# Gather, turn and scatter two experts' rows at a time: one list of 128 rows on 128 partitions

## The reference, cut to what matters

```
expert = g_sel[:, None] * EXPERTS_PER_GROUP + top_idx        # two per token
def expert_block(args):
    tok, e = args
    xb = x_pad[tok]                                          # gather rows
    hdn = jax.nn.silu(xb @ w1[e]) * (xb @ w3[e])             # 1024 -> 256
    return hdn @ w2[e]                                       # 256 -> 1024
y = y.reshape(R, D) * buf_w[:, None]                         # gate
return jnp.zeros((N + 1, D), xf.dtype).at[buf_tok].add(y)[:N]
```

## Time and profile before

| | us |
|---|---|
| median of three runs | 1641.41 |
| profiled execution, its own time | 1641.72 |
| its span | 1639.9 |
| PE busy in the span | 1408.5 |
| POOL busy in the span | 159.9 |

### The profile page before, as it was taken

The page is one execution under the profiler, slowest core; times in us unless marked ns, Lnnn a source line. Parts: engine busy times, 40 slices in busy tenths (PEclk is TensorE's granted clock), DMA queues, the critical chain, the costliest instruction groups (busy, mean ns, idle before and its releaser), DMA issues. The chain is left out here.

```text
span 1639.9 us, 21516 instructions
## 1 busy us (share of the span) xinstructions
PE 1408.5 (86%) x8567; PEld 1005.1 (61%) x8567; DVE 578.3 (35%) x1281; ACT 562.8 (34%) x1055; POOL 159.9 (10%) x193
## 2 busy tenths in 40 slices
PE   4999999999999988878797999699887879888760
PEld 4888887787888855555585888455444444444430
DVE  5455565334311415666463455211010101001007
ACT  5434444222322444454310465233222222222223
POOL 0000000000000000000000111322212121212110
PEclk9999999999999979999899999799999888899995
DMA  5101111113233300000464872999999999999977
GB/s 156 52 26 40 30 36 39 30 39 103 77 118 106 90 1 1 1 1 1 165 235 143 310 246 102 354 383 371 392 382 388 387 385 389 376 381 383 375 276 307
DMA packets 138211, 314.64 MB, mean 192 GB/s; under 512 B 32241, under 2 KB 86513, under 8 KB 120705
## 3 DMA queue, kind: packets, MB, share of 16 engines
q1 hardware_dynamic: 125056, 288.06, 49.1%
q0 software_dynamic: 13056, 25.23, 4.5%
HBM read 284.86 MB, written 43.02 MB: 200 GB/s over the span
## 5 line engine op out<-in xcount | busy, mean ns | idle before, releaser
L2031 PE MATMUL ps<-r,m_xT 128*64 128x256 f32 x2048 | 270.2, 423 | 77.7 <-DMA r<-in_w 76.4
L129 PE MATMUL ps<-uTh,h_wh 128*128 128x512 f32 (+3 forms) x696 | 264.5, 380 | 7.5 <-DVE uTl L546 7.5
L2031 PEld LDWEIGHTS ps<-r,m_xT 128*64 128x64 f32 x2048 | 158.2, 152 | 171.4 <-DMA r<-in_w 84.4
L130 PE MATMUL ps<-uTl,h_wh 128*128 128x512 f32 (+3 forms) x696 | 256.7, 369 | 0.0
L131 PE MATMUL ps<-uTh,h_wl 128*128 128x512 f32 (+3 forms) x696 | 256.5, 368 | 0.0
L129 PEld LDWEIGHTS ps<-uTh,h_wh 128*128 128x128 f32 (+1 forms) x696 | 130.1, 187 | 31.8 <-DVE uTl L546 8.3
L1993 DVE TENSOR_TENSOR m_prod<-m_sig,ps 128x128 f32<-128x128 f32 x64 | 18.4, 288 | 358.5 <-ACT m_sig L1955 278.8
L131 PEld LDWEIGHTS ps<-uTh,h_wl 128*128 128x128 f32 (+1 forms) x696 | 130.0, 187 | 20.1
L130 PEld LDWEIGHTS ps<-uTl,h_wh 128*128 128x128 f32 (+1 forms) x696 | 130.3, 187 | 19.4 <-issue 0.2
L2050 PE MATMUL ps<-r,m_hT 128*64 128x512 f32 x512 | 123.9, 605 | 0.4 <-issue 0.4
L1966 ACT ACTIVATE rows<-ps,gate 64x512 f32<-64x512 f32 x128 | 87.3, 682 | 87.1 <-PE ps L2050 85.5
(11 more groups left out here) (325 smaller groups left out, 2051.3 us busy)
## 6 DMA issues: line engine op xcount, KB each, us to landing
r<-in_w SPq DMA_DIRECT2D x192, 1024.0 KB
h_w<-in_w_in SPq DMA_DIRECT2D x37, 512.0 KB, 4.1
gates<-h_sg POOLq DMA_DIRECT2D x16, 512.0 KB, 2.9
e_gate<-gates SPq DMA_DIRECT2D x16, 512.0 KB
r<-y_moe SPq DMA_DIRECT2D x8, 1024.0 KB, 12.5
e_wo<-in_w_out SPq DMA_DIRECT2D x4, 1024.0 KB
merged<-e_m SPq DMA_DIRECT2D x8, 512.0 KB
f_m<-merged SPq DMA_DIRECT2D x8, 512.0 KB, 6.7
```

The source lines that it names most:

```text
L129: pe.matmul(out, lh, rh, start=start, stop=False)
L130: pe.matmul(out, lh, rl, start=False, stop=False)
L2031: ins = pe.matmul(bank(UP_BANK + e % 2, 0, DE, CAP * f, CAP * (f + 1)).rearrange("p (r f) -> p r f", r=2), xT[e % 2][:, j, :], g.r13[b][:, ...
```

## The change

Experts 2i and 2i + 1 become pair i. One gather brings the rows of both, the even one's on partitions 0 to 63 and the odd one's on 64 to 127; one set of eight transposes turns all 128 rows into two PSUM banks; two ACT copies take them out (one bank each); the two products stay per expert and read 64 of the 128 columns each; the results go to partitions 0 to 63 and 64 to 127 of a tile of their own, and one scatter sends both. Row tiles and result tiles are three each. DVE makes `g.src` and `g.dst` in two halves each, so the first gather waits for two instructions. Two gathers of 128 rows are issued ahead in place of three of 64. Left out below: sizes and declarations, and the same edit of `g.dst`.

```diff
-XB = 5
+XB = 3
+PAIRS = EXPERTS // 2
...
-            dve.tensor_scalar(g.src[:, :], LISTS(0, EXPERTS), SKIP, None, ALU.add).then_inc(rows_ok, 1)
+            halves = [(k, slice(k * CAP, (k + 1) * CAP)) for k in range(2)]
+            for k, part in halves:
+                dve.tensor_scalar(g.src[part, :], LISTS(0, EXPERTS)[part, k::2], SKIP, None, ALU.add).then_inc(rows_ok, 1)
...
-            for e in range(EXPERTS + 2):
+            for i in range(PAIRS + 1):
+                n = i + XB - 1
+                if n < PAIRS:
+                    if n >= XB:
+                        pool.wait_ge(x_tr, n - XB + 1)
+                    settle(pool, g)
+                    pool.indirect_dma_start(out=x[n % XB], out_offset=None, in_=g.u2,
+                                            in_offset=bass.IndirectOffsetOnAxis(ap=g.src[:, n:n + 1], axis=0),
...
+                if i >= 1:
+                    n = i - 1
+                    pool.wait_ge(y_ok, 4 * n + 4)
+                    settle(pool, g)
+                    pool.indirect_dma_start(out=g.y, out_offset=bass.IndirectOffsetOnAxis(ap=g.dst[:, n:n + 1], axis=0),
+                                            in_=y[n % XB][:, :], in_offset=None,
...
+            def copied(i):
+                act.wait_ge(x_tr, i + 1)
+                if i >= 2:
+                    act.wait_ge(up_mm, 2 * (i - 2) + 2)
+                for q in range(2):
+                    act.activation(xT[i % 2][:, 4 * q:4 * q + 4, :], bank(X_BANK + q).rearrange("p (j t) -> p j t", j=4),
+                                   ACT.Copy).then_inc(xT_ok, 1)
...
+                if e % 2 == 0 and e // 2 + 1 < PAIRS:
+                    copied(e // 2 + 1)
...
+            def turn(i):
+                pe.wait_ge(x_in[i % XB], 16 * (i // XB) + 16)
+                settle(pe, g)
+                if i:
+                    pe.wait_ge(xT_ok, 2 * i)
+                for j in range(DK):
+                    ins = pe.transpose(bank(X_BANK + j // 4, j % 4 * P, P), x[i % XB][:, j::DK], g.ident[:, :])
+                ins.then_inc(x_tr, 1)
...
-                                            xT[e % 2][:, j, :], g.r13[b][:, :, j, HALF * f:HALF * (f + 1)],
+                                            xT[i % 2][:, j, CAP * k:CAP * (k + 1)], g.r13[b][:, :, j, HALF * f:HALF * (f + 1)],
...
+                if e % 2 == 0 and e // 2 + 1 < PAIRS:
+                    turn(e // 2 + 1)
```

More of the change, by code:

```diff
@@ L1429, in output_part @@
         io8, io128, tok, upper = sb("f_io8", [P, 8]), sb("f_io128", [P, 2, EXPERTS]), sb("f_tok", [P, TT]), sb("f_upper", [P, P])
-        srcf = sb("f_srcf", [P, EXPERTS])
+        srcf = sb("f_srcf", [P, PAIRS])
         fill, xr, xr_in = g.fill, g.xrow, g.x_in
@@ L1530, in gpsimd @@
             pool.wait_ge(filled, 16 * FILLS)
-            for b in range(AHEAD):
-                pool.memset(xr[b], 0.0).then_inc(z_ok, 1)
+            for i in range(XB - 1):
+                pool.memset(xr[i], 0.0).then_inc(z_ok, 1)
             def record(t):
@@ L1543, in gpsimd @@
                 record(t)
-            pool.wait_ge(z_ok, AHEAD)
-            pool.wait_ge(rows_ok, 1)
+            pool.wait_ge(z_ok, XB - 1)
+            pool.wait_ge(rows_ok, 2)
             pool.wait_ge(u_out, 16 * TT)
             settle(pool, g)
[L1548 to L1551, removed]
+            for i in range(XB - 1):
+                pool.indirect_dma_start(out=xr[i], out_offset=None, in_=g.u2,
+                                        in_offset=bass.IndirectOffsetOnAxis(ap=g.src[:, i:i + 1], axis=0),
+                                        bounds_check=SEQ - 1, oob_is_err=False).then_inc(xr_in[i], 16)
             record(TT - 1)
@@ L1723, in vector @@
             dve.wait_ge(oh_mm, TT)
-            dve.tensor_scalar(g.src[:, :], LISTS(0, EXPERTS), SKIP, None, ALU.add).then_inc(rows_ok, 1)
-            c.mark(dve.tensor_scalar(srcf[:, :], LISTS(0, EXPERTS), SKIP, None, ALU.add))
+            halves = [(k, slice(k * CAP, (k + 1) * CAP)) for k in range(2)]
+            for k, part in halves:
+                dve.tensor_scalar(g.src[part, :], LISTS(0, EXPERTS)[part, k::2], SKIP, None, ALU.add).then_inc(rows_ok, 1)
+            for k, part in halves:
+                c.mark(dve.tensor_scalar(srcf[part, :], LISTS(0, EXPERTS)[part, k::2], SKIP, None, ALU.add))
             dve.tensor_copy(g.gate[:, :], LISTS(EXPERTS, EXPERTS)).then_inc(rows_ok, 1)
             dve.wait_ge(dv, c.now())
-            dve.scalar_tensor_tensor(out=g.dst[:, :], in0=srcf[:, :], scalar=2.0, in1=LISTS(2 * EXPERTS, EXPERTS),
-                                     op0=ALU.mult, op1=ALU.add).then_inc(rows_ok, 1)
+            for k, part in halves:
+                dve.scalar_tensor_tensor(out=g.dst[part, :], in0=srcf[part, :], scalar=2.0,
+                                         in1=LISTS(2 * EXPERTS, EXPERTS)[part, k::2], op0=ALU.mult, op1=ALU.add).then_inc(rows_ok, 1)
             dve.wait_ge(rk_mm, TT + 1)
@@ L1818, in experts_part @@
         sb = lambda n, s, d=F32: here.enter_context(nc.sbuf_tensor(n, s, d))
-        x, y, x_in = g.xrow, g.y_tile, g.x_in
-        xT = [sb(f"m_xT{b}", [P, DK, CAP]) for b in range(2)]
+        x, x_in = g.xrow, g.x_in
+        xT = [sb(f"m_xT{b}", [P, DK, P]) for b in range(2)]
         sig = [sb(f"m_sig{b}", [P, HALF]) for b in range(2)]
+        y = [g.y_first] + [sb(f"m_y{b}", [P, D]) for b in range(1, XB)]
         prod, hid = sb("m_prod", [P, HALF]), sb("m_hid", [P, HALF])
@@ L1828, in experts_part @@
         h_tr, hT_ok, dn_mm, y_ok = sem("m_h_tr"), sem("m_hT_ok"), sem("m_dn_mm"), sem("m_y_ok")
-        late_x, late_sig, late_prod, late_hid, late_y = x[0], x[1][:, 0:DE], x[2][:, 0:DE], x[3][:, 0:DE], x[4]
-        late_xT, late_hT = xT[0], hT
+        late_x, late_y = x[0][0:CAP, :], y[0][0:CAP, :]
+        late_sig, late_prod, late_hid = (t[0:CAP, 0:DE] for t in (x[1], x[2], y[1]))
+        late_xT, late_hT = xT[0][:, :, 0:CAP], hT
         rec, late_rows = sb("v_rec", [CAP, ROWS]), sb("v_rows", [CAP, ROWS], I32)
@@ L1909, in gpsimd @@
         def gpsimd(pool):
-            for b in range(AHEAD, XB):
-                pool.memset(x[b], 0.0).then_inc(x_zero, 1)
-            pool.wait_ge(x_zero, XB - AHEAD)
-            for e in range(EXPERTS + 2):
[L1914 to L1917, removed]
-                    settle(pool, g)
[L1919 to L1924, removed]
+            pool.memset(x[XB - 1], 0.0).then_inc(x_zero, 1)
@@ new lines, in gpsimd @@
+            pool.wait_ge(x_zero, 1)
+            for i in range(PAIRS + 1):
[3 more added lines that the diff above has]
+                        pool.wait_ge(x_tr, n - XB + 1)
+                    settle(pool, g)
+                    pool.indirect_dma_start(out=x[n % XB], out_offset=None, in_=g.u2,
+                                            in_offset=bass.IndirectOffsetOnAxis(ap=g.src[:, n:n + 1], axis=0),
+                                            bounds_check=SEQ - 1, oob_is_err=False).then_inc(x_in[n % XB], 16)
+                if i >= 1:
+                    n = i - 1
+                    pool.wait_ge(y_ok, 4 * n + 4)
@@ L1925, in gpsimd @@
                     settle(pool, g)
-                    pool.indirect_dma_start(out=g.y, out_offset=bass.IndirectOffsetOnAxis(ap=g.dst[0:CAP, e - 2:e - 1], axis=0),
-                                            in_=y[b], in_offset=None,
-                                            bounds_check=2 * SEQ - 1, oob_is_err=False).then_inc(y_out[b], 16)
+                    pool.indirect_dma_start(out=g.y, out_offset=bass.IndirectOffsetOnAxis(ap=g.dst[:, n:n + 1], axis=0),
+                                            in_=y[n % XB][:, :], in_offset=None,
+                                            bounds_check=2 * SEQ - 1, oob_is_err=False).then_inc(y_out[n % XB], 16)
@@ L1929, in gpsimd @@
             pool.wait_ge(g.rec_out, 32 * TT)
             for b in range(XB):
-                pool.wait_ge(y_out[b], 16 * len(range(b, EXPERTS, XB)))
+                pool.wait_ge(y_out[b], 16 * len(range(b, PAIRS, XB)))
             pool.sem_inc(v_turn, 1)
@@ L1951, in scalar @@
         def scalar(act):
-            for e in range(-1, EXPERTS + 1):
-                if 0 <= e < EXPERTS:
+            def copied(i):
[5 more added lines that the diff above has]
+                                   ACT.Copy).then_inc(xT_ok, 1)
+            copied(0)
+            for e in range(EXPERTS + 1):
+                if e < EXPERTS:
                     act.wait_ge(up_mm, e + 1)
                     act.activation(sig[e % 2][:, :], bank(UP_BANK + e % 2, 0, HALF), ACT.Sigmoid).then_inc(sig_ok, 1)
[L1956 to L1959, removed]
+                if e % 2 == 0 and e // 2 + 1 < PAIRS:
+                    copied(e // 2 + 1)
                 if e >= 1:
-                    b = (e - 1) % XB
-                    if e - 1 >= XB:
-                        act.wait_ge(y_out[b], 16 * ((e - 1) // XB))
+                    i, k = (e - 1) // 2, (e - 1) % 2
```

(23 more changed lines are left out.)

## The result

The kernel after takes 1601.15 us (median; 1599.30 to 1602.21) against 1641.34 for the kernel before: ratio 0.9754, 95% interval 0.9737 to 0.9771. It is 40 us faster, where 1642.6 and a range of 1633 to 1650 were predicted. The profiled execution took 1602.19 us, span 1600.5.

A forecast was written before the change was run, and what follows sets the result against it. The prediction took the DMA engines' stream of 201 MB of weights and the rows to bound the loop. Terms -0.6 + 1.0 + 0.5 + 0.3 = +1.2 on 1641.4 gave 1642.6 us, range 1633 to 1650.

The forecast's parts named there:

- What bounds the kernel now: Whole loop: as long as the DMA engines need for 201 MB of weights and the rows, at a share of 1.02.
- Bytes: Gathers and scatters: same rows moved, 64 transfers with their completions go; -0.6 us, gain bounded at 1.7.
- Split of a list of 128: Rows of a 128-place list dealt over 16 engines: +1 us taken, from -15 (even) to +28 (eight consecutive places).
- Transposes, ACT, POOL: Loop: PE saves 33 us in transposes, ACT copies as before, POOL saves 60 us of issues; all hidden, 0 each.
- Start: First "up" later by 0.8 to 5 us, say 3; hidden by weights already queued, so 0.
- Tail: After the last weights: last "up" possibly slower, 0 to 3.0 us, +0.5 taken; last scatter with both experts, +0.3.
- D: Rival, faster: rows go where the late engines get fewer, gain ends at 8 to 11 us, 1632 us; chance 0.10.
- E: Rival, faster: the chain's PE pieces to 1146 us are a real bound, 1634 us; chance 0.05.
- a last weight that lands over 4 us earlier: Loop's end: a sign that the forecast is wrong; if right, expert 63's weights land at about the same us.

The follow-up runs named there:

- e1: The changed kernel with each gather of 128 rows put back into two of 64, to partitions 0 to 63 and 64 to 127: 1640.38 us, ratio 0.9997.
- f3: The kernel before with separate row and result tiles, three each, and each one-expert gather naming 128 places, 64 skipped: 1600.96 us; its control, with 64-place lists, 1631.22.
- g2: The changed kernel with the places of each expert's list permuted so that filled places spread over all short runs of four: 1591.50 us, ratio 0.9706.
- g3: The kernel before with the places of each expert's list permuted so that filled places spread over all short runs of four: 1633.56 us, ratio 0.9967.
- e4: The changed kernel with every place of the gathers' lists out of range, so gathers run without rows: 1574.79 us; first weight loads left at 1019 to 1025 over all profiled runs.
- e2: The changed kernel with each scatter of 128 rows put back into two of 64, the gather staying as changed: 1595.97 us, ratio 0.9727.
- h1: The kernel before with each gather waiting until an earlier expert's rows are turned, so it leaves some 5 us after the scatter, not 1.2: 1633.26 us, ratio 0.9959.

## Why the prediction was wrong

**What bounds the kernel now**: right, it is the DMA stream, and stayed so. But I took the share of 1.02 for a full rate. I had GB/s of 383 in the earlier trace rows and made packet costs from it, without asking why other stretches at that share ran at 397 (1035 to 1040 us in the earlier trace rows) and the steps between gathers at 410 to 426.

**Bytes**, the step that failed: "the same rows are moved", priced at -0.6. The rows are the same, but what a row costs is not: I took the 0.17 us of a row and the time of a weight packet for fixed. Measured, the gathered rows cost 70 us before and 26 after: a term of -44 in place of -0.6. It had no bound below -1.7, because only the completions were bounded and not the time of the packets beside the rows. That the 64-place gather is what made them dear is shown (e1, f3); through what in the chip stays open.

**Split of a list of 128**: I asked which engine gets how many rows and not which partitions it writes. The term (+1, bounds -15 and +28) was counted in rows alone. That this pairing of engine and partition is the reason is argued, as said above. The imbalance itself is real (by the medians g2 takes 10 us from after, g3 7 from before), but the change did not remove it.

**Transposes, ACT, POOL** at 0: right. e1 has the halved turning, the copies and the joint scatter, and gains nothing; f3 has none of them, and gains all. PE is busy 1373.2 us against 1408.5, 35 less (33 forecast).

**Start**: the first "up" of after is at 1049.13 against 1044.07 in the trace of before, 5 us later (3 forecast, 0 charged); but its output part was 4 us behind already (first gather at 1038.09 against 1034.15 in the earlier trace rows), so the change's own part is about 1, and 1050 to 1055 us runs at 410 GB/s: hidden. The 4 us lie within the spread named at e4: the first weight load left SP at 1024.81 against 1021.04.

**Tail**: right. From the start of the last "up" to the end of the span after takes 58.2 us and before 57.0: 1.2 more, where 0.8 was charged, with that "up" at 5.36 in place of 3.67. So the two profiled runs differ by 3.8 us more up to the first weight load, 44.3 less from there to the last "up" (517.5 against 561.8), and 1.2 more behind it, which makes the 39.4 between their spans, but for rounding. The 44.3 is the "bytes" term again, read in another way.

**Rivals**: none had the mechanism. D and E had the sign, with 0.15, but 1632 and 1634 for reasons that are not the cause: D's rows were not relieved by the change, and E's PE chain is no bound (e1). Of the signs listed, "a last weight that lands over 4 us earlier" came true.

## What to carry to other kernels

A DMA share of 1.0 says that the engines hold packets, not that these move at full rate: compare GB/s between stretches of equal share, and a dip with the rhythm of a transfer names what to test (here gather and scatter shared the rhythm, and e2 and e3 told them apart). Where a gather shares the engines with a stream, give it a list of 128 places on all 128 partitions, even if half of them are skipped (f3: 30 us under its control). Then spread the filled places over the list (g2: up to 10 us more). Where a gather must go to half of the partitions, don't issue it right behind a scatter (h1: 5 us).

## What the runs showed of the hardware that was not expected

- A gather of 64 places into partitions 0 to 63 takes the whole stream from over 410 to between 295 and 350 GB/s in the 2.5 us step where it lands, and the DMA share shows nothing of it (1.02 to 1.04).
- Scatters out of 64 partitions cost nothing of the kind: 415 GB/s with them (e2).
- Skipped places cost little: from 1200 to 1300 us f3's row queue has 2634 packets and 9.5% of the engines' time, after's 1700 and 8.8%, and both kernels take 1601 us.
